# Value units of both sequence groups in one burst in the paged attention of a decoder trunk

## What is computed

```python
ckv_past = cache_ckv[l, page_table].reshape(b_s_dec, past, KV_RANK)   # 8 x 4096 x 256
sc = einsum('bthr,bsr->bhts', q_lat, ckv_past) + einsum('bthd,bsd->bhts', q_rope, kr_past)
pr = softmax(concat([sc, s_new]) * scale)
o_lat = einsum('bhts,bsr->bthr', pr[..., :npast], ckv_past) + ...      # the value side
...
mix = gates[0] * (h_a @ w_pa) + gates[1] * (h_b @ w_pb) + gates[2] * (h_c @ w_pc)
x = x + mix @ w_o
```

## Time and profile before

| | |
|---|---|
| Time, median of 3 runs | 2040.74 us (2039.45 to 2042.48) |
| The profiled execution: its own time, its span | 2039.3 us, 2037.6 us |
| TensorE busy | 2005.5 us, 98% of the span |
| VectorE, ScalarE, GpSimd busy | 1038.7, 709.7, 273.5 us |
| The value stretch of layer 0, of layer 1 | 318.8 to 422.6 us, 1322.5 to 1426.4 us |
| Value matmuls | 379 ns each, 1024 records |

### The profile page before, as it was taken

The page is one execution under the profiler, slowest core; times in us unless marked ns, Lnnn a source line. Parts: engine busy times, 40 slices in busy tenths (PEclk is TensorE's granted clock), DMA queues, the critical chain, the costliest instruction groups (busy, mean ns, idle before and its releaser), DMA issues.

```text
span 2037.6 us, 52983 instructions
## 1 busy us (share of the span) xinstructions
PE 2005.5 (98%) x22566; PEld 1916.2 (94%) x22566; DVE 1038.7 (51%) x1611; ACT 709.7 (35%) x1125; POOL 273.5 (13%) x520
## 2 busy tenths in 40 slices
PE   9999999999999999999999999999999999999998
PEld 9998888899999999999999998888999999999998
DVE  7876413366656444433367753224775654444323
ACT  5454114266334222222235531323652332222221
POOL 0004455500000000000000045564000000000000
PEclk9999999999999999999999999999999999999999
DMA  6428998942433323233353299999224333332332
GB/s 227 133 68 271 310 344 316 349 146 66 141 99 94 94 86 93 92 90 92 99 174 108 86 305 324 332 353 331 86 69 131 104 94 94 92 93 86 95 90 76
DMA packets 140993, 322.64 MB, mean 158 GB/s; under 512 B 24419, under 2 KB 72086, under 8 KB 140246
## 3 DMA queue, kind: packets, MB, share of 16 engines
q10 hardware_dynamic: 46944, 147.87, 23.6%
q1 hardware_dynamic: 69238, 100.05, 14.3%
q0 software_dynamic: 24576, 71.34, 10.1%
HBM read 307.08 MB, written 12.08 MB: 157 GB/s over the span
## 4 chain that ended last, share of the span: by engine, by line
PE 96%; DVE 1%; issue 1%; ACT 1%; DMA 0%; SPq 0%; ACTq 0%; DVEq 0%
PE PS L1965 28%; PE PS L1967 27%; PE PS L1966 27%; PE PS L2226 4%; PE PS L2253 3%; PE PS L2018 2%; PE PS L2385 1%; PE PS L2280 0%; PE PS L2403 0%; PE PS L2423 0%; PE PS L2004 0%; DMA xT<-in_x_t 0%; PE PS L2025 0%; DVE kxl L730 0%; PE PS L2412 0%
## 5 line engine op out<-in xcount | busy, mean ns | idle before, releaser
L1965 PE MATMUL PS<-hh,wh 128*128 128x260 f32 x3008 | 864.1, 287 | 1.6 <-DVE gtmp L1143 0.9
L1967 PE MATMUL PS<-hl,wh 128*128 128x260 f32 x3008 | 852.4, 283 | 0.7 <-issue 0.6
L1966 PE MATMUL PS<-hh,wl 128*128 128x260 f32 x3008 | 851.4, 283 | 0.5 <-issue 0.5
L1965 PEld LDWEIGHTS PS<-hh,wh 128*128 128x128 f32 x3008 | 568.9, 189 | 14.8 <-issue 6.6
L1967 PEld LDWEIGHTS PS<-hl,wh 128*128 128x128 f32 x3008 | 569.3, 189 | 0.9 <-issue 0.9
L1966 PEld LDWEIGHTS PS<-hh,wl 128*128 128x128 f32 x3008 | 568.8, 189 | 1.2 <-issue 0.9
L723 DVE TENSOR_TENSOR wl<-raw,wh 128x1024 fp32r<-128x1024 f32 (+4 forms) x326 | 351.3, 1078 | 301.5 <-ACT wh L1494 300.7
L1494 ACT ACTIVATE wh<-raw 128x1024 fp32r<-128x1024 f32 (+4 forms) x326 | 304.5, 937 | 531.6 <-PE PS L1967 526.1
L1965 PE MATMUL PS<-fh,wh 128*128 128x260 f32 x704 | 199.3, 283 | 0.0
L1967 PE MATMUL PS<-fl,wh 128*128 128x260 f32 x704 | 198.7, 282 | 0.0
L1966 PE MATMUL PS<-fh,wl 128*128 128x260 f32 x704 | 198.6, 282 | 0.0
(11 more groups left out here) (371 smaller groups left out, 2908.6 us busy)
## 6 DMA issues: line engine op xcount, KB each, us to landing
raw<-in_wpack ACTq DMA_DIRECT2D x238, 512.0 KB, 3.6
vpg<-in_cache_vals SPq DMA_DIRECT2D x256, 128.0 KB, 5.0
vpg<-in_cache_vals POOLq DMA_DIRECT2D x256, 128.0 KB, 5.0
kpg<-in_cache_keys SPq DMA_DIRECT2D x192, 144.0 KB, 4.4
kpg<-in_cache_keys POOLq DMA_DIRECT2D x192, 144.0 KB, 4.2
raw<-in_wpack ACTq DMA_DIRECT2D x48, 256.0 KB, 2.8
ky<-in_cache_keys SPq DMA_DIRECT2D x64, 144.0 KB, 4.5
raw<-in_wpack ACTq DMA_DIRECT2D x16, 384.0 KB, 3.1
```

Of the source, the lines that this page charges most:

```text
L1965: pe.matmul(out, w[0], x[0], start=first, stop=False)
L1966: pe.matmul(out, w[1], x[0], start=False, stop=False)
L1967: return pe.matmul(out, w[0], x[1], start=False, stop=last)
```

## The change

For c from 1 to 6, in both layers, `values(c, 1)` is called directly behind `values(c, 0)`. The two linears `P1c` and `g1(c+1)` then follow each other. At c = 0 and c = 7 the order stays. The loads, their order and the buffers are not touched.

```diff
--- before.py
+++ after.py
@@ -2337,6 +2337,8 @@
                     if c % 2 == 0 and c < 6:
                         turn_scores(c // 2 + 1)
                     values(c, 0)
+                    if 0 < c < 7:
+                        values(c, 1)
                     if c == 2:
                         begin("bb")
                         pe.wait_ge(*upto("lf"))
@@ -2347,7 +2349,8 @@
                     pe.wait_ge(*upto("lo hb3"))
                     linear(f"P1{c}", [f"P1{c}"], brh[1], brl[1])
                     if c < 7:
-                        values(c, 1)
+                        if c == 0:
+                            values(c, 1)
                         linear(f"g1{c + 1}", [f"g1{c + 1}"], hh, hl)
                     else:
                         linear("g00", ["g00"], hh, hl)
```

## The result

The changed kernel took 2051.57 us (median of 8 runs, 2048.21 to 2061.21) against 2043.72 us of the kernel before on the same chips (8 runs). The ratio is 1.0047, with a 95% interval from 1.0025 to 1.0069. It is slower by 0.5%: 9.6 us by the ratio, 7.9 us between the medians. That is outside the range that was forecast. A second timing of the same two kernels gave 1.0034 (1.0019 to 1.0048), 2048.90 us of 12 runs against 2041.16 us of 35. The profiled execution is the slowest of the first eight, 2061.21 us.

What follows compares the result with a forecast made beforehand. TensorE was taken as the bound, with pages just in time behind it. A 3.7 us saving against 3.7 us of waits at (6,1) left 2039.3 us profiled, forecast as a 2040.7 us median, range 2037.3 to 2044.3.

Steps and rivals of the forecast that it cites:

- The saving: Each burst of two value units on TensorE saves 0.31 us; twelve over two layers save 3.7 us.
- Where the wait would be: TensorE waits at (6,1) for unit 55, in front of the 33rd record: 1.8 and 1.9 us in the two layers.
- with the same distance unit 55 lands at 399.7: Unit 55's last transfer keeps landing 14.4 us after the reading of (5,0), so (6,1) waits 1.8 us.
- the sum: Waits at (6,1) of 3.7 us against a saving of 3.7 us: 0.0 us of change; chance 0.40.
- nothing lands sooner than before: Upper end for the waits at (6,1): 3.0 and 3.1 us, making the sum +2.4 us.
- What it costs nothing: Weights of `g1(c+1)`, wanted 1.8 us sooner, and PSUM banks add no cost; VectorE and ScalarE have over half their time free.
- (5,1) and the others: Unit 45 lands at 385.5, just when (5,1) wants to start; a short wait there would move no end.
- All three signs of being wrong: (7,0) starting over 1 us off, TensorE waiting at an eighth before the fifth, stretch windows with a clock under 1.00.
- The limit of the memory: About 358 GB/s per core from HBM would mean no sooner landings and +2.4 us; not taken for the sum.
- The rival built on it: Transfers are the bound: landings of (6,1) stay where they were, time +2.4 us; chance 0.15.
- The clock: Rival: waits at (6,1) halve TensorE's clock, 1.5 us per fall; one or two falls 0.18, three or more 0.07.
- A: Theory after the result: `P15`'s 512 KB weight load, issued 1.7 us later, delays unit 55; distance 17 us instead of 14.4.

Runs made afterwards that it cites:

- the stretch without waits: Changed kernel loading a quarter of the bytes for units 54 and 55; stretches 101.3 and 100.7 us, without the waits both 100.5 us.

## Why the prediction was wrong

**The saving** was right. 2.28 us for a lone unit and 1.73 for a second one gave 0.31 us, and the stretch without waits confirmed it. The seam inside a burst, where nothing waits, was the 0.20 us of the lower bound.

**Where the wait would be** was right, and so was its form: (6,1) in both layers, in front of the 33rd record. The rest of the row on GpSimd kept its distance as I had said, 9.0 us from the last start of (5,0) to the last issue of unit 55.

**The step that failed** is "with the same distance unit 55 lands at 399.7", and the reason given for it, that the 14.4 us "are mostly issues of that engine in a fixed order behind one release". Of the 14.4 us only 9.0 are issues. The other 5.4 us are the flight of the last transfer, and it took 8.1 us in layer 0 and 7.7 in layer 1. The distances were 17.1 and 16.9 us, and with the 0.14 us from the landing to the start, which the sum had left out, the waits of 1.8 and 1.9 us became 4.65 and 4.4 us. I had bounded them from above by "nothing lands sooner than before", 3.1 us of wait, and both lie outside. The cause stood in the prediction under "What it costs nothing". There I counted for the moved linears what VectorE and ScalarE do, but not the transfer that ScalarE issues with it. `P15` ends 1.7 us later against the release of (5,0), and so the 512 KB load behind it goes out at 5.3 us and not at 3.6. Holding it back gives the loss back; moving it in the kernel before gives 0.8 and 1.6 us of the 2.7 and 2.4. The waits came to 10.2 us and not 3.7, and the clock, which the sum had at nothing, added 4.2 us: 10.2 + 4.2 - 3.7 is the +10.8 us of the two stretches, to 0.1 us.

**(5,1) and the others.** No wait came at (5,1) in either profile of the changed kernel, where the sum had left 0.0 us to spare in layer 0. In the first one 0.4 us at (1,1) and 0.7 us at (4,1) in layer 1 were not forecast; they were absent the second time. All three signs of being wrong were there: (7,0) started over 5 us late against (0,0) in layer 0, TensorE waited at an eighth before the fifth, and windows of the stretch had a clock under 1.00.

**The limit of the memory.** The trace still goes above the 358 GB/s of the Trainium skill's page "DMA: Bandwidth & Descriptors", section "Where 436 GB/s comes from": 401 and 410 GB/s from 399 to 410. The rival built on it, landings that don't move, was nearer than my sum in its sign, and too small: unit 55 landed 3.7 us later than before on the time axis of the trace, whose stretch started 2.2 us later. From the start of the stretch that is 1.5 us later (2.3 us in layer 1), where the rival had no change and my sum 1.2 us sooner.

**The clock.** The rival was right in mechanism and in the price of a stretch at half speed: 1.6 us for 3.4 us, about half of them value matmuls, against an estimate of 1.5 us, and 2.6 us for 6.8 us, of which the first 1.1 us still lay in the wait. The clock fell once in each layer, in both profiles, which I had given 0.18 as one or two falls. But in layer 0 it stayed low for twice the 3.4 us that I had priced, so the cost was that of the three falls that I had given 0.07. They came with the waits of 4.65, 4.4, 3.9 and 3.3 us of the changed kernel, but not with those of 3.7 and 3.3 us of bursts at 5 and 6 alone, nor with that of 2.5 us where all loads behind `P1c` were held back. What decides between these isn't settled.

**What stays open** is the size of A: why a shift of 1.7 to 1.9 us costs 0.8 and 1.6 us in the kernel before and 1.3 to 2.7 us in the changed one. The spread between two executions of one kernel is 0.7 and 1.1 us for the changed one and 0.3 and 1.5 us for bursts 1 to 4, so with one or two executions of each the two ranges can't be parted. Every wait of over 2.5 us at (6,1) came with this load in its late place, and with this load alone held back none there was over 1.3 us. That its shift alone makes the whole delay is not shown. A kernel with this weight load cut to a few bytes, which would have measured its bytes apart from its place, wasn't run.

## What to carry to other kernels

Where a linear is moved, the transfers that go out at its end move with it, even if the weights in them are used over 12 us later: look at what they meet in flight. A distance from a release to a landing has a part that is issue and a part that is flight, and here only the first kept its length when something else was shifted. In a stretch where the DMA engines are near full, a load with much slack is one to try holding back: here it gave back the loss of the rearrangement (1.0034 became 1.0004), though neither gained anything that can be measured on the kernel before.

## What the runs showed of the hardware

The same transfer of 128 KB took from 4.2 us to 8.1 us from issue to landing, with the same transfers on its own queue, in kernels that differ in the bursts and in where one weight load of 512 KB on another engine's queue stood. With that load held back the last transfer landed after 4.2 us, but the engines moved 334 and 345 GB/s at that place, so the load isn't what keeps the rate under 400. Windows of the changed kernel with the load held back, timed, at the same distance from (5,0) as those from 391 to 399 above:

```profile
390.33:394.33 4.00, 4.00 (x36) 4.00 (x36) 1.02 (x2) 1.06 (x1) 2.58 (x6) 1.00 0.98 334
394.33:398.33 4.00, 4.00 (x36) 4.00 (x34) 0.90 (x1) 0.00 (x0) 2.66 (x6) 1.00 0.97 345
```

And in the changed kernel a second weight load of 512 KB was in flight from 401.11 for 8.5 us, while the engines moved 407 GB/s, at a DMA share of 1.03:

```profile
401.11 0.34 ACTq L687 DMA_DIRECT2D raw<-in_wpack  x1
```

What sets the rate in these windows isn't shown. The clock fell to half with four waits of 3.3 to 4.65 us between two groups of value matmuls, and stayed with two others of 3.3 and 3.7 us. It fell in none of the bursts without a wait, which last 3.3 us from first start to last.
